# Transposed up-projection in the second block kind: weights held in the array, hidden rows streamed past them

## The reference

```python
D_FF_2 = 4 * D_MODEL            # 4096

def rms_norm_2(x, g):
    xf = x.astype(jnp.float32)
    y = xf * lax.rsqrt(jnp.mean(xf * xf, axis=-1, keepdims=True) + NORM_EPS)
    return (y * g.astype(jnp.float32)).astype(x.dtype)

def hybrid_layer(...):
    ...
    x = x + jnp.sum(gates * proj, axis=2) @ w_o

    hf = rms_norm_2(x, g_ffn)
    x = x + jnp.square(jax.nn.relu(hf @ w_up)) @ w_down
    return x
```

## Time and profile before

| | |
|---|---|
| median of three runs | 1566.56 us (1565.55 to 1568.37) |
| the profiled execution | 1566.81 us, of which the span of its instructions is 1565.0 us |
| TensorE busy | 1478.0 us, 94% of the span |
| VectorE, ScalarE, GpSimd busy | 936.6, 796.1 and 173.6 us |
| one block of 512 hidden columns, with its transposes | 11.79 us |

### The profile page before, as it was taken

One profiled execution on the slowest core, in us unless ns is written; L12 is line 12 of the kernel. 1 busy time (PEld: TensorE's weight loads), 2 busy tenths in 40 slices (PEclk: granted clock), 3 DMA queues, 4 the chain that ended last, 5 costly groups with the idle time before them and its releaser, 6 DMA issues.

```text
span 1565.0 us, 21417 instructions
## 1 busy us (share of the span) xinstructions
PE 1478.0 (94%) x6967; PEld 1211.0 (77%) x6967; DVE 936.6 (60%) x1038; ACT 796.1 (51%) x970; POOL 173.6 (11%) x156
## 2 busy tenths in 40 slices
PE   2998899999998899999999999999999999999997
PEld 1777688787776788787878888888778788888885
DVE  3684555544684555454577886654446788766544
ACT  3665445434564445445566555553355665455432
POOL 0536100000545000000030000000001200000000
PEclk9999899999999899999999999999999999999998
DMA  7343365554542565465444475546553545655541
GB/s 270 129 141 108 108 215 166 196 174 138 162 136 81 162 190 184 147 202 178 136 156 154 161 234 198 170 153 218 186 164 112 168 141 184 234 188 169 185 157 40
DMA packets 158753, 258.03 MB, mean 165 GB/s; under 512 B 9330, under 2 KB 60604, under 8 KB 158524
## 3 DMA queue, kind: packets, MB, share of 16 engines
q1 hardware_dynamic: 154048, 250.48, 48.9%
q10 hardware_dynamic: 4604, 6.31, 1.3%
HBM read 255.71 MB, written 1.05 MB: 164 GB/s over the span
## 4 chain that ended last, share of the span: by engine, by line
PE 47%; issue 41%; POOL 5%; DVE 3%; ACTq 1%; ACT 1%; POOLq 0%; DVEq 0%
PE bank L462 14%; PE bank L464 14%; PE bank L463 14%; PE bank L481 3%; POOL stat L1989 2%; ACTq L891 1%; POOL decay L2015 1%; DVE w_lo L1387 1%; PE bank L544 1%; POOL junk L2013 1%; POOL proj L2023 0%; PE bank L711 0%; POOL cst L2078 0%; POOL proj L2054 0%; DVE proj L1569 0%
## 5 line engine op out<-in xcount | busy, mean ns | idle before, releaser
L1387 DVE TENSOR_TENSOR w_lo<-w_raw,w_hi 128x2048 fp32r<-128x2048 f32 (+1 forms) x251 | 555.5, 2219 | 235.1 <-ACT w_hi L924 230.0
L924 ACT CAST w_hi<-w_raw 128x2048 fp32r<-128x2048 f32 (+1 forms) x251 | 455.4, 1824 | 229.3 <-PE bank L464 223.8
L462 PE MATMUL bank<-w_hi,hT_hi 128*128 128x512 f32 (+1 forms) x1376 | 550.3, 400 | 19.4 <-DVE hT_lo L1416 6.6
L464 PE MATMUL bank<-w_hi,hT_lo 128*128 128x512 f32 (+1 forms) x1376 | 540.4, 393 | 0.0
L463 PE MATMUL bank<-w_lo,hT_hi 128*128 128x512 f32 (+1 forms) x1376 | 539.7, 392 | 0.0
L462 PEld LDWEIGHTS bank<-w_hi,hT_hi 128*128 128x128 f32 x1376 | 261.6, 190 | 78.4 <-issue 22.8
L464 PEld LDWEIGHTS bank<-w_hi,hT_lo 128*128 128x128 f32 x1376 | 261.2, 190 | 55.0
L463 PEld LDWEIGHTS bank<-w_lo,hT_hi 128*128 128x128 f32 x1376 | 261.8, 190 | 50.7
L1989 POOL TENSOR_TENSOR stat<-stat,cst 128x2 f32<-128x2 f32 (+3 forms) x23 | 41.0, 1782 | 1121.4 <-DVE stat L1436 978.8
L462 PE MATMUL bank<-w_hi,hid2T_hi 128*128 128x512 f32 x256 | 101.6, 397 | 0.0
L463 PE MATMUL bank<-w_lo,hid2T_hi 128*128 128x512 f32 x256 | 101.1, 395 | 0.0
(11 more groups left out here) (244 smaller groups left out, 1417.0 us busy)
## 6 DMA issues: line engine op xcount, KB each, us to landing
w_raw<-in_w_gate SPq DMA_DIRECT2D x108, 512.0 KB, 4.0
w_raw<-in_w_up SPq DMA_DIRECT2D x108, 512.0 KB, 4.7
w_raw<-in_w_down SPq DMA_DIRECT2D x104, 512.0 KB, 4.5
w_raw<-in_w_in SPq DMA_DIRECT2D x88, 512.0 KB, 4.4
w_raw<-in_w_out SPq DMA_DIRECT2D x16, 512.0 KB, 4.2
w_raw<-in_w_branch SPq DMA_DIRECT2D x32, 256.0 KB, 3.0
w_raw<-in_w_o SPq DMA_DIRECT2D x16, 512.0 KB, 4.7
bgate<-in_b_gate ACTq DMA_DIRECT2D x16, 256.0 KB, 3.4
```

The source lines that it names most:

```text
L462: pe.matmul(o, hi[:, kt, rows_of(r)], w_hi[:, s, j, 0:cols], start=begin, stop=False)
L464: mm = pe.matmul(o, lo[:, kt, rows_of(r)], w_hi[:, s, j, 0:cols], start=False, stop=end)
L924: act.copy(w_hi[:, s, 0:kts, :], w_raw[:, s, 0:kts, :]).then_inc(hi_ready, 1)
L1387: dve.tensor_tensor(w_lo[:, s, 0:kts, :], w_raw[:, s, 0:kts, :], w_hi[:, s, 0:kts, :].bitcast(F32), ALU.subtract).then_inc(lo_ready, 1)
```

## The change

In the second kind's up-projection the operands change places. A slab is now 1024 rows by 256 columns of w_up (`narrow` gives that view of the same memory), one slab to a block of 256 hidden columns, and `UPS` = 16 blocks a layer. `hidden` holds 128 x 128 of w_hi and streams hT_hi and hT_lo side by side, 512 columns in one matmul; the same for w_lo with hT_hi alone, 256 columns. In a bank, columns 0 to 255 collect w_hi hT_hi + w_lo hT_hi, and columns 256 to 511 w_hi hT_lo. The result is the hidden part already transposed, so `turn_hid2` and its copies are gone.

ScalarE copies the right halves of both banks to SBUF (`cross`), VectorE adds them to the left halves (`hidden_sum`), frees the banks, and forms max(s, 0) * s in one instruction; ScalarE rounds to hid2T_hi (`hidden_hi`), VectorE subtracts for hid2T_lo (`hidden_lo`). Since rows now lie along the free dimension, rstd isn't applied there; its square (one tiny VectorE instruction into stat) multiplies the result of w_down when it is added to x (`add_down`). hT_hi and hT_lo become halves of one tensor. The first two blocks are interleaved around the transposes of x.

```diff
-                for i in q.rounds(4, dict(slab=4)):
-                    for b in range(2):
-                        for k0 in (0, 4):
-                            slab(*rows(w["w_up"], k0, 4, i * (2 * NB) + b * NB, NB))
+                for i in q.rounds(UPS // 4, dict(slab=4)):
+                    for b in range(4):
+                        src = w["w_up"][:, bass.ds(i * (2 * NB) + b * HALF, HALF)].rearrange("(c p) n -> p c n", p=P)
+                        slab((lambda s: narrow(s)[:, 0:4, :], src[:, 0:4, :]),
+                             (lambda s: narrow(s)[:, 4:8, :], src[:, 4:8, :]))
...
-                first_block(slab_product)
-                for _i in q.rounds(3, dict(slab=4, blk=2, turn=4)):
-                    for _ in range(2):
-                        wide_block()
-                        turn_hid2(q.now("blk") - 1)
-                wide_block()
-                earlier, last = q.now("turn"), q.now("blk")
-                turn_hid2(last - 1)
-                pe.wait_ge(turn_free, earlier + 2)
+                def hidden(a, slab, kts):
+
+                    hi, lo = narrow(w_hi[:, slab]), narrow(w_lo[:, slab])
+                    for kt in kts:
+                        for n in range(2):
+                            o, cols = a[n], slice(n * P, (n + 1) * P)
+                            if kt:
+                                pe.matmul(o[:, 0:SEQ], lo[:, kt, cols], hT_hi[:, kt, :], start=False, stop=False)
+                            mm = pe.matmul(o[:, :], hi[:, kt, cols], hT[:, :, kt, :], start=kt == 0, stop=kt == KT - 1)
+                            if not kt:
+                                pe.matmul(o[:, 0:SEQ], lo[:, kt, cols], hT_hi[:, kt, :], start=False, stop=False)
+                    if kt == KT - 1:
+                        mm.then_inc(slab_used, 1)
...
+                all_turned()
+                last = q.now("blk")
+                first = [(open_block(), up_slab())]
+                hidden(*first[0], range(0, 4))
+                read_out(last)
+                turn_x(1)
+                first.append((open_block(), up_slab()))
+                hidden(*first[1], range(0, 4))
+                for g in range(2):
+                    pe.wait_ge(turn_free, q.now("turn") + 1 + g)
+                    for opened in first:
+                        hidden(*opened, range(4 + 2 * g, 6 + 2 * g))
+                for _ in range(2):
+                    hidden_block()
+                for _i in q.rounds(UPS // 4 - 1, dict(slab=4, blk=4)):
+                    for _ in range(4):
+                        hidden_block()
...
+                def cross():
+                    used(1)
+                    a = block_of()
+                    for n in range(2):
+                        ins = act.copy(cross2[:, n, :], a[n][:, SEQ:2 * SEQ])
+                    ins.then_inc(cross_ready, 1)
+
+                def hidden_hi(at, j):
+                    act.wait_ge(hid_ready, q.next("hid"))
+                    act.copy(hid2T_hi[:, bass.ds(at, 2), :], sum2[j % 2][:, :, :]).then_inc(hid_hi, 1)
...
+                def hidden_sum(j):
+                    used(1)
                     a = block_of()
+                    dve.wait_ge(cross_ready, q.next("hid"))
+                    for n in range(2):
+                        ins = dve.tensor_tensor(sum2[j % 2][:, n, :], a[n][:, 0:SEQ], cross2[:, n, :], ALU.add)
+                    ins.then_inc(acc_free, 1)
+                    dve.wait_ge(acc_free, q.now("blk") + 2)
+                    dve.scalar_tensor_tensor(sum2[j % 2][:, :, :], sum2[j % 2][:, :, :], 0.0, sum2[j % 2][:, :, :],
+                                             ALU.max, ALU.mult).then_inc(hid_ready, 1)
...
+                def add_down(b, signals=1):
...
+                        ins = dve.scalar_tensor_tensor(x[:, r, b * NB:(b + 1) * NB], a[r][:, :],
+                                                       stat[:, S_X2 + r:S_X2 + r + 1],
+                                                       x[:, r, b * NB:(b + 1) * NB], ALU.mult, ALU.add)
```

More of the change, by code:

```diff
@@ L191, in build @@
         x = sb("x", [P, R, D])
[L192 to L193 removed]
+        hT = sb("hT", [P, 2, KT, SEQ], F32R)
+        hT_hi, hT_lo = hT[:, 0], hT[:, 1]
         cst = sb("cst", [P, C_W])
@@ L334, in rows_of, with narrow @@
             return slice(r * P, (r + 1) * P)
+        def narrow(slab):
+            return slab.rearrange("p k (h c) -> p (k h) c", h=2)
         @block.sync
@@ L868, in _, with up_slab @@
-                wide_block()
-                earlier, last = q.now("turn"), q.now("blk")
-                turn_hid2(last - 1)
-                pe.wait_ge(turn_free, earlier + 2)
+                def up_slab():
+                    pe.wait_ge(lo_ready, q.next("slab") + RING)
+                    return (q.index("slab") - 1) % RING
+                def hidden(a, slab, kts):
[10 more added lines that the diff above has]
+                        mm.then_inc(slab_used, 1)
@@ new lines, in hidden_block @@
+                def hidden_block():
+                    a = open_block()
+                    hidden(a, up_slab(), range(KT))
+                all_turned()
[10 more added lines that the diff above has]
+                        hidden(*opened, range(4 + 2 * g, 6 + 2 * g))
@@ L874, in _ @@
                     for n in range(8):
-                        if (b, n) == (0, 6):
-                            all_turned()
+                        if b == 0:
+                            pe.wait_ge(hid_lo, q.next("hid", 2))
                         slab_product(a, hid2T_hi, hid2T_lo, range(4 * n, 4 * n + 4), NB, n == 0, n == 7)
-                        if (b, n) == (0, 0):
-                            turn_hid2(last)
                         if b == 1 and n == 1:
@@ L1961, in _ @@
+                for i in q.rounds(UPS // 4, dict(loop4, blk=4, hid=4)):
+                    for j in range(4):
+                        hidden_sum(j)
+                        split_lo()
+                        hidden_lo(i * 8 + 2 * j, j)
+                for _ in range(UPS):
+                    next(ahead)
+                root()
+                step(dve.tensor_tensor(stat[:, S_X2:S_X2 + 2], stat[:, S_XR:S_XR + 2], stat[:, S_XR:S_XR + 2], ALU.mult))
+                splits(9)
                 used(8)
-                add_x(0)
+                add_down(0)
@@ L1966, in _ @@
                 used(8)
-                a = block_of()
-                for r in range(R):
-                    ins = dve.tensor_tensor(x[:, r, NB:D], x[:, r, NB:D], a[r][:, :], ALU.add)
-                ins.then_inc(acc_free, 2)
+                add_down(1, 2)
                 q.next("blk")
```

93 lines of the change are left out of this document (30 added, 63 removed).

## The result

The changed kernel takes 1557.51 us (median of five runs, 1557.12 to 1558.11) against 1566.56 us (1563.15 to 1568.37) before: a ratio of 0.9945 with a 95% interval of 0.9930 to 0.9959, 0.55% faster. The prediction was 1558.0 us. The median of before is that of five runs here, the three known at the prediction among them, and came out the same. The profiled execution of the changed kernel took 1558.11 us with a span of 1556.2 us, 8.8 us less than the 1565.0 of the earlier trace rows.

The account below looks back on a forecast made before the run. TensorE's matmuls times their pace bound the stage: 14.1 us of transposes go, 4.2 us return as narrow products, 1.0 + 0.26 us are lost, 8.7 us net. From 1566.81 us that gives 1558.1, stated as 1558.0; 8-in-10 range 1551 to 1566 us.

Parts of the forecast that it names:

- What bounds: Up-projection: time is number of matmuls times their pace, TensorE busy 94.36 of 94.36 us, if other engines keep up.
- The transposes, 14.1 us: Up-projection: 16 sets of eight transposes at 0.88 us each, all on the path, go away.
- The narrow product, 0.122 us: Up-projection: each 256-column product of w_lo with hT_hi takes 0.122 us, bounds 0.109 and 0.133, far end 0.173.
- The wide product, 0.2272 us: Up-projection: each 512-column product of w_hi with both parts keeps the earlier kernel's pace of 0.2272 us.
- The wait before the third block, 0.5 us a layer: Start of up-projection: TensorE waits about 0.5 us for the first block's banks, once a layer, 1.0 us in all.
- The additions to x, 0.13 us a layer: After the down-projection: multiply-adds from PSUM take 0.746 instead of 0.682 us, two waited for, 0.26 us in all.
- VectorE and ScalarE at no cost: Up-projection: VectorE needs 4.9 us and ScalarE 3.2 us of a 5.58 us block, so neither adds time.
- DMA rows of 1 KB at no cost: Up slabs: memory rows of 1 KB instead of 2 KB, priced at nothing since slab memory is free some 17 us early.
- Bare loads: Up-projection rival: loads not covered by narrow products, step 0.19 us, 34.8 us more, 1593 us; chance 7%.
- Lockstep: Up-projection rival: VectorE and ScalarE finish a block's whole chain before the next begins, 13 us, 1571 us; chance 5%.
- Two runs of the stream: Up-projection rival: wide product reading two runs 8 KB apart costs a few ns, 1561 to 1567 us; shared chance 13%.
- A narrow step between 0.133 and 0.173 us: Up-projection rival: 256-column product slower than forecast, e.g. 0.139 us, 1561 to 1567 us; shared chance 13%.

Follow-up runs that it names:

- the run with 128 columns: Changed kernel with half of the w_lo product left out, streaming only the first 128 rows of hT_hi: 1554.11 us in one run.
- the all-narrow run: Changed kernel with each wide up-projection product made as two of 256 columns with the same stationary piece: 1562.40 us, ratio 0.9977.
- the run with 0.6 us more work: Changed kernel with one more VectorE maximum over 128 x 512 constants in each up-projection block: 1558.18 us, ratio 0.9950.
- the one-run layout: Changed kernel with hT_hi and hT_lo of a k chunk side by side, so the wide product streams one run of 512 columns: 1556.55 us.

## Why the prediction was right, step by step

- **What bounds.** TensorE's matmuls times their pace, with no gaps: held in the changed kernel too, but for one wait a layer. With VectorE busy 89% of the stage it still held; with VectorE busy throughout, VectorE was the bound. Between the two nothing was tried.
- **The transposes, 14.1 us.** Put back alone they cost 0.89 us a set; the term was 0.88.
- **The narrow product, 0.122 us, bounds 0.109 and 0.133.** Among its own kind it takes 0.120 us, just the 106.7 ns of streaming and the surcharge of the wide ones in the kernel before. The line through 384 columns gave 0.119 us and was right to 1 ns; the one through 420 gave 0.133, since products of 420 columns take 0.192 us, 4 ns above their streaming and that surcharge. The choice of 0.122 was 2 ns too high. The floor of 0.109 us from the transposes fits the run with 128 columns and lies just below.
- **The wide product, 0.2272 us.** Taken over unchanged; in the mix its step reads 0.2333 us and the narrow one's 0.1166. The term that the sum used, 0.349 us a pair, measured 0.350. This is partly luck: I had no ground for the pair but the sum of two kinds measured alone, which with 0.120 would have been 0.347. Every other block goes at just that, 5.56 us for 16 pairs; the others, at 5.63, are slower for a reason that stays open, and the 2 ns too many for the narrow one made up for them.
- **The wait before the third block, 0.5 us a layer.** 0.36 us in the step, and 0.37 to 0.42 us by the stage without it. The prediction had 0.74 us for ScalarE's two copies, which took 0.65, and 0.96 us for VectorE's two additions, which took 0.75.
- **The additions to x, 0.13 us a layer.** 0.12 us.
- **VectorE and ScalarE at no cost, and DMA rows of 1 KB at no cost.** Both held; VectorE has 1.4 us a block to spare by its steps (5.6 - 4.2), where the prediction had 0.7.
- **The last step of the sum.** 1558.1 less 0.25 is 1557.9, not 1558.0; that changes nothing.
- **The rivals.** Bare loads: excluded by the all-narrow run. Lockstep: excluded by the run with 0.6 us more work. Two runs of the stream: excluded by the one-run layout, at least above 0.1 us a layer. A narrow step between 0.133 and 0.173 us: excluded by the 0.120 measured.

## What to carry to other kernels

Where the transposed form of a result is what the next product needs, make it so from the start by exchanging the operands: the streamed columns are the same, and the transposes go for the price of more, narrower products. That price can be read from the pace of products that are there, from start to start and over a whole period of unlike matmuls, not from durations or single steps. Then look whether equal forms go at unequal paces in different places: here 6 ns a matmul by the start of a tensor were worth 7.8 us, nearly as much as the whole change.

## What the runs showed of the hardware

- The start of the stationary operand's rows matters: 32 bytes off a multiple of 64, a product of 512 columns (fp32r) steps at 0.2332 to 0.2336 us instead of 0.2266 to 0.2274, shown by moving one region onto the multiple and another off it. Products of 384 and 420 columns didn't show it (0.173 and 0.176 us, 0.192 and 0.190 us).
- With a load of 128 x 128 for each, fp32r products of 256 columns step at 0.120 us and those of 512 at 0.227 us. The 256 columns between them take 107 ns, which is one column a cycle at 2.4 GHz; 13 to 14 ns come on top. The 0.173 us of 384 columns fit that, the 0.192 us of 420 columns are 4 ns more. Going from 256 to 128 columns saves 8.4 ns a pair and not 53: a product with its load doesn't get much shorter than 0.11 us.
- The noted start of a matmul can lie before the end of its load's row: 0.13 us before it behind a product of 128 columns, with the missing time in the next step.
- A streamed operand in two runs 8 KB apart costs no more than one run (0.2333 and 0.2337 us a step).
- VectorE's instructions over 512 to 2048 columns follow each other 0.08 us sooner than their rows are long.
